# Making the low parts of two weight chunks in one vector operation, in the wide stages of a decoder layer

## The reference, cut to what matters

```python
proj = rms_norm(h, mix_norm_pre) @ w_in            # 2048 x 15,488: q, kv, z, x, B, C, dt, two gates
attn = mla_branch(...)                             # latent attention, 16 heads
ssm = mamba2_branch(...)                           # chunked scan, 64 heads
mixed = sigmoid(g_attn) * (attn @ w_attn_o) + sigmoid(g_ssm) * (ssm @ w_ssm_o)
h = h + rms_norm(mixed @ w_out, mix_norm_post)
f = rms_norm(h, ffn_norm_pre)
f = (silu(f @ w_gate) * (f @ w_up)) @ w_down       # 2048 x 5632, twice, and 5632 x 2048
h = h + rms_norm(f, ffn_norm_post)
h = h + rms_norm((p @ w_ple) * sigmoid(rms_norm(h, ple_norm_pre) @ w_ple_gate), ple_norm_post)
```

## Time and profile before

| what | value |
|---|---|
| median of 3 runs | 1994.02 us (1993.68 to 1994.37) |
| profiled execution, first to last instruction | 1992.0 us; the page gives no other time for it |
| PE busy | 1979.0 us, 99% |
| PEld busy | 1681.0 us, 84% |
| DVE busy | 1668.8 us, 84% |
| ACT busy | 1147.6 us, 58% |
| mean granted TensorE clock | 0.999 |
| HBM traffic | 387 MB read, 198 GB/s over the span |
| L1914 (low part of a chunk) | 559 operations, 662.5 us |

### The profile page before, as it was taken

The page is one execution under the profiler, slowest core; times in us unless marked ns, Lnnn a source line. Parts: engine busy times, 40 slices in busy tenths (PEclk is TensorE's granted clock), DMA queues, the critical chain, the costliest instruction groups (busy, mean ns, idle before and its releaser), DMA issues.

```text
span 1992.0 us, 29428 instructions
## 1 busy us (share of the span) xinstructions
PE 1979.0 (99%) x10149; PEld 1681.0 (84%) x10149; DVE 1668.8 (84%) x2336; ACT 1147.6 (58%) x1482; POOL 18.9 (1%) x37
## 2 busy tenths in 40 slices
PE   9999999999999999999999999999999999999998
PEld 8888888888888888998888888888888888888886
DVE  7788888889888868767777787999999988888887
ACT  6666566666655545565545565556555555555575
POOL 0000000000000000000000000000000000000000
PEclk9999999999999999999999999999999999999999
DMA  8666676666566566545556667666566666766754
GB/s 235 200 191 190 190 206 184 188 192 195 172 207 209 189 203 223 156 132 156 191 191 239 205 207 242 189 202 202 190 201 200 200 201 201 254 201 207 244 189 152
DMA packets 255197, 394.74 MB, mean 198 GB/s; under 512 B 28840, under 2 KB 161440, under 8 KB 252928
## 3 DMA queue, kind: packets, MB, share of 16 engines
q1 hardware_dynamic: 251104, 369.87, 59.7%
q0 software_dynamic: 3824, 23.43, 3.5%
q10 hardware_dynamic: 176, 0.20, 0.0%
HBM read 387.08 MB, written 6.36 MB: 198 GB/s over the span
## 4 chain that ended last, share of the span: by engine, by line
PE 98%; DVE 1%; ACT 0%; DMA 0%; issue 0%; DVEq 0%; SPq 0%; ACTq 0%
PE acc L655 16%; PE acc L851 15%; PE acc L853 15%; PE acc L852 15%; PE acc L660 8%; PE acc L912 6%; PE acc L913 6%; PE acc L914 6%; PE acc L1107 1%; PE acc L785 1%; PE acc L637 1%; PE acc L636 1%; PE acc L638 1%; PE acc L1038 1%; PE acc L1242 0%; PE acc L714 0%
## 5 line engine op out<-in xcount | busy, mean ns | idle before, releaser
L1914 DVE TENSOR_TENSOR wlo<-raw,whi 128x1024 fp32r<-128x1024 f32 (+2 forms) x559 | 662.5, 1205 | 110.8 <-ACT whi L1351 108.3
L1351 ACT ACTIVATE whi<-raw 128x1024 fp32r<-128x1024 f32 (+1 forms) x560 | 572.2, 1044 | 244.4 <-PE acc L853 81.7
L655 PE MATMUL acc<-u,whi 128*128 128x512 f32 x1376 | 328.7, 391 | 0.0
L851 PE MATMUL acc<-whi,u 128*128 128x512 f32 x824 | 323.0, 392 | 0.1
L853 PE MATMUL acc<-whi,u 128*128 128x512 f32 x824 | 320.8, 389 | 0.0
L852 PE MATMUL acc<-wlo,u 128*128 128x512 f32 x824 | 320.6, 389 | 0.0
L655 PEld LDWEIGHTS acc<-u,whi 128*128 128x128 f32 x1376 | 252.7, 188 | 48.8
L851 PE MATMUL acc<-whi,g 128*128 128x512 f32 x520 | 202.8, 390 | 0.1
L853 PE MATMUL acc<-whi,g 128*128 128x512 f32 x520 | 202.4, 389 | 0.0
L852 PE MATMUL acc<-wlo,g 128*128 128x512 f32 x520 | 202.3, 389 | 0.0
L1374 ACT ACTIVATE whi<-raw 128x1024 fp32r<-128x1024 f32 x72 | 76.5, 1062 | 209.9 <-PE acc L914 162.0
(11 more groups left out here) (597 smaller groups left out, 2990.8 us busy)
## 6 DMA issues: line engine op xcount, KB each, us to landing
raw<-w_in_in SPq DMA_DIRECT2D x208, 512.0 KB, 3.8
raw<-w_gate_in SPq DMA_DIRECT2D x176, 256.0 KB, 3.0
raw<-w_up_in SPq DMA_DIRECT2D x176, 256.0 KB, 3.3
raw<-w_down_in SPq DMA_DIRECT2D x88, 512.0 KB, 4.6
raw<-w_ssm_o_in SPq DMA_DIRECT2D x64, 512.0 KB, 4.3
raw<-w_in_in SPq DMA_DIRECT2D x64, 256.0 KB, 4.0
raw<-w_attn_o_in SPq DMA_DIRECT2D x32, 512.0 KB, 4.7
raw<-w_out_in SPq DMA_DIRECT2D x32, 512.0 KB, 4.9
```

Of the source, the lines that this page charges most:

```text
L655: return T.matmul(bank(banks[i]), wh[:, j, i * P:i * P + P], src[:, kts[j], :, :].rearrange("p a s -> p (a s)"), start=start and j == 0, s ...
L851: T.matmul(o, x_hi, wh[:, j, :], start=start, stop=False, skip_group_check=True)
L1351: S.activation(whi[:, slot, 0:w], raw[:, slot, 0:w], ACT.Copy).then_inc(sem("hi_ready"), 1)
L1914: V.tensor_tensor(wlo[:, slot, 0:w], raw[:, slot, 0:w], whi[:, slot, 0:w].bitcast(F32), ALU.subtract) \
```

## The change

A new tuple `PAIRED` names four stages, `so`, `ao`, `ff` and `dn`. In `wide_low`, a plain chunk of these stages no longer gets its low part at its own place: nothing is issued for the even chunk, and at the odd chunk one operation (`pair_low`) subtracts over both slots, 2 x 1024 columns, after waiting for the high part of the odd chunk, and raises `lo_ready` by 2. Stages outside the tuple (`wo`, `pg`) keep `split` for plain chunks. The chunks of `so` and `ao` ahead of `PAIRS_AT` go the same way, two by two. In `seven_sums`, in all wide stages, the low part of the two inner halves (1024 columns) and that of the last half (512) become one operation of 1536 columns, at the place of the second; `lo_ready` goes up by 2 there. ScalarE's and TensorE's programs and the loads are as before.

```diff
+PAIRED = ("so", "ao", "ff", "dn")
@@ seven_sums
             inner = slice(CHUNK * slot + 512, CHUNK * slot + 512 + CHUNK)
+            three = slice(CHUNK * slot + 512, CHUNK * slot + 2 * CHUNK)
             V.tensor_tensor(t[:, 0:2, :], raw_f[:, inner].rearrange("p (a n) -> p a n", a=2),
                             raw[:, slot, 0:512].unsqueeze(1).to_broadcast([P, 2, 512]), ALU.add) \
                 .then_inc(sem("t_sum"), 1)
-            dve.wait_ge(sem("hi_ready"), num(phase, it, c) + 1)
-            V.tensor_tensor(wlo_f[:, inner], raw_f[:, inner], whi_f[:, inner].bitcast(F32), ALU.subtract) \
-                .then_inc(sem("lo_ready"), 1)
             dve.wait_ge(sem("t_sum"), 3 * n + 1)
             V.tensor_tensor(t[:, 2, :], t[:, 0, :], raw[:, slot + 1, 0:512], ALU.add).then_inc(sem("t_sum"), 1)
             dve.wait_ge(sem("t_sum"), 3 * n + 2)
             V.tensor_tensor(t[:, 3, :], t[:, 2, :], raw[:, slot + 1, 512:], ALU.add).then_inc(sem("t_sum"), 1)
             dve.wait_ge(sem("hi_ready"), num(phase, it, c + 1) + 1)
-            V.tensor_tensor(wlo[:, slot + 1, 512:], raw[:, slot + 1, 512:], whi[:, slot + 1, 512:].bitcast(F32),
-                            ALU.subtract).then_inc(sem("lo_ready"), 1)
+            V.tensor_tensor(wlo_f[:, three], raw_f[:, three], whi_f[:, three].bitcast(F32), ALU.subtract) \
+                .then_inc(sem("lo_ready"), 2)
@@
+        def pair_low(phase, it, c):
+
+            slot = c % RING - 1
+            dve.wait_ge(sem("hi_ready"), num(phase, it, c) + 1)
+            V.tensor_tensor(wlo[:, slot:slot + 2, :], raw[:, slot:slot + 2, :], whi[:, slot:slot + 2, :].bitcast(F32),
+                            ALU.subtract).then_inc(sem("lo_ready"), 2)
+
         def wide_low(phase, it, c, between=None):
 
-            if not is_seven(phase, it, c):
+            if is_seven(phase, it, c):
+                if c % 2 == 0:
+                    seven_sums(phase, it, c, between)
+            elif phase not in PAIRED:
                 split(phase, it, c)
-            elif c % 2 == 0:
-                seven_sums(phase, it, c, between)
+            elif c % 2:
+                pair_low(phase, it, c)
```

## The result

| | before | after |
|---|---|---|
| time, us (median; lowest to highest) | 1993.85 (1993.63 to 1994.37), 4 runs | 2033.96 (2033.34 to 2039.63), 4 runs |
| ratio of times | | 1.0207, 95% interval 1.0192 to 1.0221 |
| profiled execution, us | | 2034.12, span 2032.5 |

What follows compares the result with a forecast made beforehand. PE bound the kernel, busy 99% of the span. Stalls of 10.7 + 3.7 + 2.5 + 5.4 + 4.9 + 4.9 + 1 = 33 us, taken as 32, added to the 1994.0 median gave 2026 us, range 2008 to 2042.

Steps and rivals of the forecast that it cites:

- the weights: Paired slots' loads go out together, the first later; block-product slots return in 10.3 us, PE needs 10.2: 1 us.
- Ready time of a plain pair: Later of vector engine free and second chunk's high part done + 0.03, plus 2.285 us; some 36 places lack room.
- ff, chunks 0 to 3: Low parts of chunks 0 and 1 0.48 us late, chunks 2 and 3 behind the product 1.19; nine turns, 10.7 us.
- ff, chunk 6 and chunk 14, turns 1 to 4: Late high parts stall PE 0.93 us at chunk 6 and 0.5 at chunk 14 per turn: 3.7 and 2.0 us.
- so, ao, dn: Stalls at single chunks of these stages, such as behind gates, evacuations or late weights: 5.4, 4.9 and 4.9 us.
- Block-product pair, 0.06 us later, nothing: Chain to the second low part 4.34 us instead of 4.28; 0.3 us of room nearly everywhere, so no cost.
- Vector busy time down by 30 us: On the vector engine, 206 fewer operations: 31 us by durations, 14 us where chained; off the path, costed at nothing.
- Rival A: PE's lead over a pair hides the change: 1994 +- 3; 4 in 100.
- B: Faster: vector engine full, 14 to 31 us of its time go; at best 1991; 3 in 100.
- C: Two loads at once take 7 us; each of 72 block-product pairs costs 0.6 to 1 us: 2066; 9 in 100.
- D: Stalls overlap more, so only ff's nine turns and so remain: 10.7 + 4 = 2009; 14 in 100.
- The rule weighed: Group operations if the vector engine is saturated; break them up if it is not but causes bubbles elsewhere, the forecast's case.

Runs made afterwards that it cites:

- the last experiment: Kernel before with the 2048-column operation only for 38 plain pairs in steady middles of so, ao, ff and dn: 1994.71 us, ratio 1.0005.
- half loads: Only the first half of the columns of each so, ao, ff, dn weight load: changed kernel 2026.74 us; kernel with only the block-product merge 1994.31 us.
- the gate moved: Changed kernel with ff's gate and product of the turn before placed after chunk 3 instead of chunk 2: 2027.53 us, ratio 1.017.
- the control with half loads: Kernel before with only the first half of the columns of each so, ao, ff and dn weight load: 1993.76 us, ratio 0.9999.

## Why the prediction came out 8 us short

The mechanism was right and one term, the weights, was mis-sized. In some others the sum was nearer than its parts.

- **Vector time is cover, not path** (forecast: worth nothing). Nothing contradicts it: where the merge costs nothing, in the last experiment, it also brings nothing. But there the page shows no vector time won either, so it was not put to a hard test.
- **Price of the two shapes** (2.285 and 1.751 us by the line through two sizes). 2.289 and 1.751 measured.
- **Ready time of a plain pair** (later of the vector engine's free time and the second high part, and then 2.285 us). Right in its form: 34 of the 40 us go when each half has its own operation and signal, some 30 of them without the late weights. The runs also separate what the forecast had in one: waiting for the second half (its operation and its high part) is nearly the whole price, and the later start alone, together with the merged operation of the block products, costs about 6 us with its late weights.
- **ff, chunks 0 to 3** (1.19 a turn, nine turns, 10.7 us). 1.15 to 1.18 in all nine, and without the product ahead of the pair chunk 2 lost nothing in any of them. By the forecast that was worth 9 x (1.19 - 0.48) = 6.4 us, and the time fell by 6.4; but it is 8.0 at the place and 1.6 lost elsewhere, so the agreement is in part luck. The 0.48 at chunk 0 shows as its own stall in turns 6 to 10 alone. Turns 2 to 5 follow a turn that stalled at chunk 14, and there PE reaches chunk 0 later; the sum of a turn is the same, but in turns 2 to 5 all of it hung on the product.
- **ff, chunk 6 and chunk 14, turns 1 to 4** (0.93 and 0.5). 0.95 to 1.03; 0.49 to 0.51 with half loads, 0.47 to 0.91 with full ones: the excess is weights.
- **so, ao, dn** (5.4, 4.9, 4.9). ao 5.0, place by place. dn without weights: 1.18, 0.85, 1.23, 0.63 and 1.23 = 5.1. In so the sum was near by luck (6.2, of it 1.3 weights), for its parts were not: chunk 8 lost 1.0 instead of 2.3 and chunk 18 lost 1.6 instead of 0.3. I took chunk 9's late weights from the trace of before as fixed; the loads landed otherwise in this run (and with the gate moved chunk 8 lost 0.4). Chunk 18 is a wait that the forecast had wrong. Half loads leave it, so it isn't the weights' size, and the two traces show what it is, though no run tried it by itself. Between the high parts of chunks 18 and 19 ScalarE makes so_gate, which waits for PE's chunk 15. Before, ScalarE came to it later than PE was done; after, it waits for PE:

```profile
597.01 1.28 ACT L1574 ACT_TABLE_LOAD   x1
```

```profile
598.44 1.28 ACT L1575 ACT_TABLE_LOAD   x1 [1.66 <-PE acc L854]
```

So the gate and the high part of chunk 19 slip by 1.4 us with PE's earlier stalls (2.0 us up to there), which the forecast had let hide nearly all of this one.

- **Block-product pair, 0.06 us later, nothing.** Right: with half loads the 72 pairs cost 0.4 us, within the interval of no change.
- **Weights** (1 us, bounds 0 and 8). This is the term that failed, though within its bounds: 7.2 us in after. The block products alone cost 4 in their own kernel; taking their merge out of after gave back 2.7 (2033.96 against 2031.28). I reckoned the mean round of a pair's slots (10.3 us against 10.2) and found it all but hidden. The mean was fine: no row of equal stalls runs through the middles. What costs are single late landings, which the 0.6 to 0.9 us of room of a pair don't cover; the control with half loads shows that in the kernel before the ring still covered them. With 7.2 in place of the 1, the forecast's sum of 33 becomes 39 of the 40 us.
- **Vector busy time down by 30 us.** Right for the durations, wrong for the page's busy time. Added up in the traces, all operations of the vector engine took 1803.9 us before and 1775.9 after, 28.0 less, and the low parts alone 811.9 and 781.6, 30.2 less. But the page's busy time is not the sum of the spans: a moment in which two operations overlap counts once (535 times 1.218 is 651.6 us, and the earlier trace rows has 641.1). So counted it fell by 3.4 us only the earlier trace rows, less than the forecast's lower bound of 14; the overlap shrank from 135.1 to 110.5 us. With the block products' merge alone the page's time even rose, to 1670.4: the second sum, which had a low part ahead of it and overlapped its end, now starts 0.03 us after the end of the sum that it needs (1294.36 + 1.22 = 1295.58, and 1295.61). With the plain pairs' merge alone it fell to 1665.7. Nothing in the time hangs on it.
- **Rival A** (hidden) and **B** (faster) are out by the result. **C** (weights decide, at each of the 72 pairs): there are late weights, but at a dozen places that differ from one execution to the next, not at each pair; 7 us, not 40. **D** (stalls overlap): they don't, since with half loads, almost free of late weights, 33 us remain, and 32 were added up for the stalls alone.
- **The rule weighed** (the Trainium skill, "Perfetto Trace Analysis", Optimizing Scalar/DVE Operations). The runs bear out its second half: the vector engine, at 84%, does not set the path, larger operations won nothing, and two operations in place of the one gave back 34 us. The vector engine's fixed part per chained operation was again 0.07 us where two stand back to back (two of 1024 columns 2.35 us, one of 2048 2.28); over all 206 merges the page's busy time shows far less, 3.4 us.

## What to carry to other kernels

When two operations of a producer are merged, price the consumer's *first* need, not the producer's saving: the first half is late by the whole second half, by its operation (here 1.07 us) and by the wait for its input. With the later place behind other work that made some 33 us at some 36 places, and 7 more in late weights. The saving, at most 0.07 us each, would count only if the producer were on the path, which no run here has. Split signals are worth more than fewer instructions wherever the consumer's lead is below one operation; look for such places at the edges of stages, not in the steady middle, by laying ready time against first use pair by pair. And a merged operation also frees its buffers together, and the first of them later: the loads behind it lose their stagger and some of their lead, which shows in single late landings and in a wider spread of times rather than in a mean.

## What the runs showed that I had not expected

- The weights' cost lies in the spread and not in the mean. The median time to landing of dn's loads hardly moved (4.6 us in the earlier trace rows, 4.4 after), and the one late pair alone cost 2.05 us:

```profile
raw<-w_down_in SPq DMA_DIRECT2D x88, 512.0 KB, 4.4
```

- A stall shows differently by view. 40 us of added time are 42.3 us as waits of the weight loads on the two merged operations and 25.3 us as waits of matmuls, with the busy time of PE up by 15.5 us.
